# Where a small expert gives way to a large one, its last down units are fetched and multiplied ahead of the large one's first gate and up units

## What is computed

```python
logits = (t @ router_w)
top_v, top_i = lax.top_k(logits, 2)
...
for e in range(N_EXPERTS):
    out = out + gates[:, e:e + 1] * swiglu(t, w_gate[e], w_up[e], w_down[e])
...
def swiglu(t, w_gate, w_up, w_down):
    return (jax.nn.silu(t @ w_gate) * (t @ w_up)) @ w_down
```

## Time and profile before

| what | value |
|---|---|
| time, median of 3 runs (lowest, highest) | 2566.37 us (2565.43, 2566.4) |
| time of the profiled execution | 2566.91 us |
| its span in the trace | 2565.1 us |
| mean granted clock of TensorE, share of full speed | 0.972 |
| PE busy | 2332.2 us (91%) |
| weight loads busy | 1647.4 us (64%) |
| DVE busy | 1662.3 us (65%) |
| ACT busy | 918.7 us (36%) |
| POOL busy | 605.9 us (24%) |
| read from the chip's memory | 821.35 MB |

### The profile page before, as it was taken

How to read it: one execution, slowest core, us unless ns; L and a number is a source line. 1 busy time by engine, 2 the same in 40 slices (tenths; PEclk the granted TensorE clock), 3 DMA queues, 4 the chain that set the end, 5 groups by cost and what they waited for, 6 DMA issues and landing times.

```text
span 2565.1 us, 31544 instructions
## 1 busy us (share of the span) xinstructions
PE 2332.2 (91%) x11714; PEld 1647.4 (64%) x11714; DVE 1662.3 (65%) x2928; ACT 918.7 (36%) x1372; POOL 605.9 (24%) x580
## 2 busy tenths in 40 slices
PE   5999999998999999899899989998998998877777
PEld 4789998787874786587578557576874544322222
DVE  6867995775951872494287025447578788787875
ACT  3234443334741761473175022012323333332332
POOL 0000000000034444454345400000023443433331
PEclk9999999998999999999999989999999999999999
DMA  9555866454999999999999973125469999999997
GB/s 366 213 215 224 328 270 262 164 230 159 361 363 421 419 353 421 421 370 404 421 417 352 421 294 140 64 99 228 183 269 350 420 421 420 420 422 421 421 421 291
DMA packets 108768, 824.54 MB, mean 321 GB/s; under 512 B 11896, under 2 KB 14200, under 8 KB 15360
## 3 DMA queue, kind: packets, MB, share of 16 engines
q0 software_dynamic: 79200, 576.75, 54.9%
q1 hardware_dynamic: 28688, 243.45, 24.7%
q10 hardware_dynamic: 720, 2.25, 0.3%
HBM read 821.35 MB, written 1.05 MB: 321 GB/s over the span
## 4 chain that ended last, share of the span: by engine, by line
PE 65%; DMA 17%; DVE 10%; issue 5%; ACT 2%; SPq 0%; POOL 0%; DVEq 0%; ACTq 0%; POOLq 0%
PE ps L733 9%; PE ps L735 8%; PE ps L734 8%; DMA ring<-in_uv,arena 8%; PE ps L719 8%; PE ps L797 6%; PE ps L1108 6%; PE ps L1594 4%; DMA arena<-in_uv,arena 4%; PE ps L752 4%; PE ps L1125 2%; DMA ring<-in_moe_w_down,arena 2%; DMA ring<-in_moe_w_gate,arena 2%; DMA ring<-in_moe_w_up,arena 2%; PE ps L727 1%
## 5 line engine op out<-in xcount | busy, mean ns | idle before, releaser
L2398 ACT ACTIVATE arena_r<-ring 128x2048 fp32r<-128x2048 f32 x210 | 402.7, 1918 | 71.0 <-DMA ring<-in_moe_w_gate,arena 40.8
L1952 DVE TENSOR_TENSOR ring_r<-ring,arena_r 128x2048 fp32r<-128x2048 f32 x168 | 385.2, 2293 | 33.0 <-ACT arena_r L2398 27.7
L1594 PE MATMUL ps<-ring,sel 128*128 128x512 f32 x568 | 272.1, 611 | 65.9 <-ACT sel L2398 65.4
L2398 ACT ACTIVATE arena<-ps 128x256 f32<-128x256 f32 (+2 forms) x238 | 109.3, 459 | 545.6 <-PE ps L727 219.8
L2918 POOL DMA_INDIRECT ring<-in_uv,arena x142 | 133.7, 942 | 596.5 <-DVE arena L2218 351.5
L1594 PE MATMUL ps<-arena,sel 128*128 128x512 f32 x456 | 221.5, 614 | 48.3 <-ACT sel L2398 47.1
L2398 ACT ACTIVATE sel<-cs,arena 128x128 f32<-128x128 f32 x256 | 102.8, 401 | 415.3 <-DVE arena L2349 327.3
L1594 PEld LDWEIGHTS ps<-ring,sel 128*128 128x128 f32 x568 | 100.9, 190 | 215.3 <-ACT sel L2398 132.8
L1108 PE MATMUL ps<-ring,arena 128*64 128x256 f32 x1792 | 203.8, 382 | 9.0 <-DMA ring<-in_moe_w_up,arena 5.5
L2371 DVE CUSTOM_DVE_ANT_0 accb<-ring,ps 128x1024 f32<-128x1024 f32 x142 | 173.4, 1221 | 49.5 <-DMA ring<-in_uv,arena 46.3
L733 PE MATMUL ps<-arena_r,h_r 128*128 128x512 f32 x448 | 180.7, 403 | 18.8 <-ACT arena_r L2398 9.3
(11 more groups left out here) (315 smaller groups left out, 4352.6 us busy)
## 6 DMA issues: line engine op xcount, KB each, us to landing
ring<-in_ada_w SPq DMA_DIRECT2D x24, 1024.0 KB, 10.2
ring<-in_ada_w SPq DMA_DIRECT2D x12, 2048.0 KB, 8.1
ring<-in_w_in SPq DMA_DIRECT2D x10, 2048.0 KB, 12.6
ring<-in_w_ada SPq DMA_DIRECT2D x8, 2048.0 KB, 7.8
ring<-in_ffn_w_gate SPq DMA_DIRECT2D x14, 1024.0 KB, 5.5
ring<-in_ffn_w_up SPq DMA_DIRECT2D x14, 1024.0 KB, 6.9
ring<-in_ffn_w_down SPq DMA_DIRECT2D x14, 1024.0 KB, 7.2
ring<-in_moe_w_gate SPq DMA_DIRECT2D x14, 1024.0 KB, 5.0
```

What stands on the lines that cost most here:

```text
L1594: last = e.matmul(ps.banks[2 * t + c], m.diag[:, i % NDIAG, :], rows[:, 1024 + 512 * c:1536 + 512 * c], start=(i % 128 == 0), stop=(i % 12 ...
L1952: v(e.tensor_tensor(ring_low[ring.half[unit]], ring.buf[unit], mo.high[unit_at[unit] % NHIGH].bitcast(F32), ALU.subtract), ("low", unit))
L2398: A.mark(e.activation(out, src, func, **kw), name)
```

## The change

At the three seams (steps 14, 28 and 42 of the first turn) the last down unit of the small expert moves ahead of the wide expert's first gate and up units: in the order of the fetches, on PE, and on ACT, where the copy `act_high` that the down matmuls wait for moves from behind the first three high parts to ahead of them. Nothing is added or left out, DVE's code is the same, and the number of transfers and instructions is the same.

```diff
+def down_first(turn, i):
+    return turn == 0 and i % 14 == 0 and 0 < i < 56
...
         def moe_units(turn):
             for i in range(57):
+                last = [("md", turn, i - 1, h) for h in range(2) if i]
+                if down_first(turn, i):
+                    yield from last
                 if i < 56:
                     for w in ("mg", "mu"):
                         for h in range(2):
                             yield w, turn, i, h
-                if i:
-                    for h in range(2):
-                        yield "md", turn, i - 1, h
+                if not down_first(turn, i):
+                    yield from last
...
+                    if down_first(turn, i):
+                        down(i - 1)
                     first("mg", i)
...
                     first("mu", i)
...
-                    if i:
+                    if i and not down_first(turn, i):
                         down(i - 1)
...
-                    if i:
+                    if i and not down_first(turn, i):
                         act_high(i - 1)
...
                     emptied(("mg", turn, i))
+                    if down_first(turn, i + 1):
+                        act_high(i)
                     if i < 55 and wide_next:
                         high("mg", i + 1, 0)
```

## The result

The changed kernel takes 2578.16 us (median of 6 runs, 2576.3 to 2580.66) where the kernel before takes 2566.39 us (6 runs, 2563.69 to 2570.02): a ratio of 1.0046, 95% interval 1.0033 to 1.0059, or +11.8 us. It is slower, by 0.46% and clear of the noise. The time lies in the predicted range of 2572 to 2587, and 3.9 us under the predicted 2582.1. The profiled execution took 2580.24 us with a span of 2578.4, 13.3 us over the one before.

A forecast was written before the change was run, and what follows sets the result against it. PE's wide-expert delay at each seam was taken to persist, through buffers and fetches, into the byte-bound stretch. Seams +12.7 us, first clock drop 0, second +3.0: +15.7 on 2566.9 us, 2582.6, or 2582.1 as median; range 2572 to 2587.

The forecast's parts named there:

- The landing: At the three seams the first gate half lands later behind the down halves: +4.97, +4.98 and +4.67 us.
- The down matmuls: At the seams, PE's 3.6 us of down matmuls move into its wait for the gate half and cost nothing there.
- What they leave behind: Behind step 14's last up matmul, only 0.65 us of 3.6 is gained; the rest becomes a wait for DVE.
- The first clock drop: Behind PE's wait for the gate half: loss stays 6.3 us in all, 0 change, bounds -6.3 to +1.2.
- The second clock drop: Behind the new gaps after step 14: 1.5 us a drop, at two of three seams, +3.0 us (0 to 4.5).
- Rival D: Gaps behind step 14 leave the clock alone while the 12.7 us delay stands: 2579.1 us, chance 0.25.
- POOL's queue: Transfers behind the seam wait for buffers returned some 4 us later, but ten buffered halves cover 25 us: cost nothing.
- A: The wide expert's late start is made good before 960 us: no change, 2566.4 us, or 2574 half absorbed; chance 0.10.
- E: The change doesn't do what it says at the seams; no size, given no chance.
- B: At the seams the down halves land without pushing the gate back: 2.0 us gained, up to 6.3 more, 2558 us; chance 0.05.
- C: The clock holds at the seams and behind step 14: 12.7 - 6.3 = +6.4 us, 2572.8 us; chance 0.07.
- The sum: Over the three seams, late landings less the gains: 4.32, 4.33 and 4.01 us, together +12.7; +15.7 with the clock.

The follow-up runs named there:

- e1: Changed kernel with PE and ACT back in the order of the kernel before, so only the fetch order is new: 2582.49 us, ratio 1.0061.
- e3: Changed kernel with DVE's low part of the next step's first gate half put ahead of step 14's product (likewise at later seams): 2571.76 us, ratio 1.0022.
- e7: Kernel before with only DVE's low part of the next step's first gate half put ahead of step 14's product: 2566.34 us, ratio 1.0000.
- e9: The changed kernel run again unaltered, for the spread of its seams: 2579.22 us, ratio 1.0046 to the kernel before.
- e10: The changed kernel unaltered, a third profile for the clock drops at its seams: 2576.89 us (one run).
- e4: Changed kernel with the change kept at the first seam only: 2571.95 us, ratio 1.0018 to the kernel before.
- e2: Kernel before with the new order on PE and ACT alone, fetches in the old order: 2592.60 us, ratio 1.0098.
- e8: Kernel before with the large expert's first gate unit fetched one unit earlier and step 12's down unit multiplied behind it: 2564.65 us, ratio 0.9991.

## Why the prediction was right, point by point

The delay and where it comes from were right; the clock's share was not, and the total came out 3.9 us too high (+15.7 forecast, +11.8 measured).

**The landing** was right at all three seams: ACT starts on the first gate half 4.97, 4.99 and 4.68 us later, against 4.97, 4.98 and 4.67. e1 shows it to be the cause.

**The down matmuls** cost nothing in the wait, as said. The wait came back behind them at 5.0 us, predicted 4.7.

**What they leave behind** was right: 0.68 us gained against 0.65 predicted, the rest turned mostly into 0.93 and 1.70 us of waiting (predicted 0.85 and 2.0); the second wait is for DVE's queue, as e3 and e7 show.

**The first clock drop** was put at no change from 6.3 us, at most 1.2 more. It is 6.9 us in the first profile of the changed kernel, 7.9 in e9 and 6.2 in e10: no change within the spread, but the upper bound was too narrow. Its longest drop was that of one profile; in the control e7, without the change, PE works 5.9 us at the lower clock at the second seam, where that profile has 3.0.

**The second clock drop** is the term that was mis-sized. I took it at two of three seams, +3.0 us. It came at one of the three seams of the first profile (1.7 us), at none of the six in e9 and e10, at the one of e4, and at one of the three of e2, which has the same two gaps of 0.93 and 1.70 us (below, its third seam): three of thirteen.

```profile
1320.90:1324.30 3.40, 3.40 (x10) 0.50 1.01 393
```

The row on which I leaned, 590.9 to 594.3 us, has 1.7 us of idle time, less than the 2.6 us of the new gap, and was no good model for it all the same. Three in thirteen makes some 1.2 us for three seams instead of 3.0. Rival D, which left the term out, gives 2579.1 us, 0.9 from the median; its rule, that of the Trainium skill (TensorE: Matmul & The Clock Gate, Why this matters for your kernels), agrees with ten of the thirteen seams and not with the other three.

**POOL's queue** was put at nothing, since the ring was "nearly all on its way". The bytes do run low for a while. In the changed kernel POOL has a gap between 852 and 860 us, and the transfers run low from 875 to 880 us, where they moved 426 GB/s before (stretches with all engines, then PEclk, DMA share, GB/s; the changed kernel's):

```profile
875.00:880.00 5.00, 5.00 (x26) 4.12 (x25) 4.53 (x4) 2.52 (x2) 2.59 (x2) 1.00 0.70 238
```

It has no price of its own that the ruler shows in the large expert: from step 16 to 25 the displacement is constant. At steps 26 and 27, where PE waits for bytes again, 0.8 us is added (4.43 to 5.24 us), but this is not shown to be the change's doing: the same kernel adds 0.3 us there in e9 and in e10, with the transfers at 301 GB/s from 875 to 880 us in e9, and e8 adds 0.8 with 421 GB/s in that stretch. Late in the large expert (894.4 to 964.4 us) the rate is 347 GB/s, under 357, as the prediction said.

**The rivals.** A (absorbed) falls by e4 and by the constant displacement. D (no second drop, 2579.1 us) came nearest, though the second drop did come now and then. E (the change doesn't do what it says) falls, as the rows above show all three moves. B (faster) asked for a gate half less than 0.65 us late; it was 4.97. C (no clock drop) didn't occur at any of the ten changed seams of the first profile, e4, e9 and e10: each had a first drop.

**The sum.** Landing less the gain is 12.6 us as measured, 12.7 as predicted. The three seams came to 16.5, 15.7 and 12.7 us in the three profiles; the medians of the whole say 11.8 and 11.6 us. So of the 3.9 us that the forecast was too high, the second drop explains about 1.8. The other 2 us stay open: the wait for the gate half and the gap behind step 14 are the same in all three profiles. That the seams of the ruler add up to more than the medians is in part the choice of the one profile that it starts from, which reaches step 11 later than nine of the eleven others. That the time fell well inside the range confirms the delay by the landings, not the two clock terms.

## What to carry to other kernels

A queue of transfers that is always full is a schedule: a unit of two halves that moves ahead costs each half that it passes two places, here 4.97 us, even if the unit itself is used in time that was idle. So what needs work between landing and use, here the halves that must be split, should not be pushed back for what an engine could use at once. To move it further ahead is another matter: e8 did, and isn't shown to gain. And before work is taken away from behind an instruction, look for what it covers: 3.6 us of matmuls gave back 0.7.

## What the runs showed of the hardware that was not expected

Two gaps of 0.93 and 1.70 us, with 0.63 us of transposes between them, were followed by a drop of the granted clock to 0.5 in three of thirteen cases and by none in the others, though these waits were the same to 0.1 us. A wait of 5.0 us was followed by one at all ten changed seams of the first profile, e4, e9 and e10. At the first seam of the changed kernel PE worked from 3.1 to 5.3 us at the lower clock behind it, a loss of 1.6 to 2.7 us; at the second seam of the kernel before and of its control it was 3.0 and 5.9 us. So profiles of one kernel differ by some microseconds for no reason that its code shows.
